# A two-layer block on one core: the end of a projection in another order, one gate's table later, four sums on GpSimd

## The chip, the core and the metric

One core of a Trainium2 chip runs the whole program in one launch. Its engines are TensorE (PE), VectorE (DVE), ScalarE (ACT) and GpSimd (POOL), each with its own list of instructions; SyncE (SP) issues most DMAs, POOL and ACT issue the others. The metric is the device time of one execution in microseconds (us).

## The reference, cut to what matters

The first layer makes 4096 columns of mixed features `y` for 512 tokens, in two halves of 2048 (`y_a` from a state space scan, `y_b` from a gated product), projects them with `w_out` and normalises:

```python
y_a = _rmsnorm(y * jax.nn.silu(z_ssd), g_ssd)
sg = jnp.einsum('gqk,bckgd->bcqgd', w_s, vn) + jnp.swapaxes(b_s, 0, 1)[:, :, None]
y_b = _rmsnorm(u * sg.reshape(bsz, L, MLP_W) * jax.nn.silu(z_mlp), g_mlp)
mixed = jnp.concatenate([y_a, y_b], axis=-1) @ w_out      # 512x4096 @ 4096x2048
out = _rmsnorm(mixed, g_post[l])
x = x + gate[:, None] * out
```

The second layer normalises this `x` again and begins with its own projections.

## The kernel before, in words

All matmuls of size work on float32 numbers split in a high and a low part: ACT writes the high part of a weight tile (`WH`, 128x1024), DVE the rest (`WL`, raw minus high), and TensorE makes three products, high by high, high by low, low by high. Four buffers `WH[n % 4]`, `WL[n % 4]` go round: unit n can be made when TensorE has used unit n-4. `make(u)` in ACT's and DVE's programs makes unit u's part.

**The projection.** K is cut in four blocks of 1024 (`c` = 0 to 3), and the columns in two halves (`q` = 2c + n). For seven of the eight pairs, `q` = 0 to 6, the 2x2 block product is made by Strassen's scheme in the form of Winograd: seven products (`ph` = 0 to 6) in place of eight. One `product(q, ph)` is 24 matmuls of 128x128 by 512 columns, over two units of weights, and it comes in two halves `j` (token blocks), each in a bank of its own. I write (q, ph) for it below. Weight forms (`E`, `F`, `H`, `G`) are sums of raw tiles: `add_load` on POOL issues a DMA from DRAM that adds to the tile in SBUF, as soon as DVE has taken the earlier form's low part from that tile (event `lo`). In POOL's list the order of a group is F, H, G, and then E of the next group, two issues each.

The left side needs forms of `y`: `F` holds the four blocks A11, A21, A12, A22 of one `c`, and four sums of 128x1024, `sum_S(c, 1..4)`, are made in `E0` and `E1s` on DVE: S1 = A21 - A22, S2 = S1 - A11, S4 = A12 + S2, S3 = A11 - A21. ACT splits off the high part (`form_high`, `FH`), DVE the low part (`form_low`, `FL`). Tables (`forms_due`, `sums_due`, `tiles_due`) say in which slot (q, ph) of the engines' lists each stands. In an even group the third sum S3 stands in slot (q, 2) and its form 5 in slot (q, 3); in an odd group S1, S2 and S4 of the next block stand in slots 3, 5 and 6. SP loads the next `y` (`load_y`, eight DMAs F<-SY) when the last forms of the block before have been made, form 6 among them; ACT then scales its tiles.

After each half product its bank is added to `O` in SBUF (`evacuate`, on DVE or, in eight cases, on ACT). The first group also holds the last two of the 16 gates of the first layer. A gate is: SP loads `vg`, `wsg`, `bsg`; DVE scales `wsg` into the table `wsr`; TensorE multiplies it with `vg` (line L841, written `sg`); DVE finishes `sgt` and `evb`; ACT stores them and squares; DVE adds to `GA`. The steps are generators in a queue `bg2`, advanced by `step(bg2, n)`. Gate 15's `wsr` was made in DVE's slot (0, 2), and its matmuls came right after product (0, 2).

**The tail.** The eighth pair is done plainly: eight units `tail_unit(0..7)`, the first four for column block 2 (order: unit, then token block k), the last four for column block 3 with k outermost, so that token block k is complete one after the other. `take_out(nb, k)` adds such a bank to `O`; `square_out(k, nb)` on ACT squares a quarter of a token row block for the norm; `gain(k, nb)` on DVE multiplies by the table `gg`. Then for each k comes the chain `take_out(3, k)`, square, `rx` on POOL, `make_x1` (x + gate * norm), square again, `rx2` on POOL, scale into `XR` (`xs2`). TensorE's transposes of `XR` (L967, `turn_row`) open the second layer. In the loop over `i` of the tail, each step first makes unit i + 2.

Of the kernel before, what the change touches and what calls it, by code (L numbers as in the profile page):

```python
# [153 lines left out]


def sums_due(q, ph):

    c = q // 2
    if q == 0:
        return {0: [(0, 2), (0, 4)], 2: [(0, 3)]}.get(ph, [])  # L160
    if q % 2:
        return [(c + 1, i) for i in {3: [1], 5: [2], 6: [4]}.get(ph, [])]
    return [(c, 3)] if ph == 2 else []
# [320 lines left out]
def tensor_program(P, m, s, ev):  # L484
# [407 lines left out]
    def product(q, ph):  # L892
        for j in range(2):
# [19 lines left out]
            if q == 0:  # L913
                step(bg2)

    for q in range(GROUPS):
        for ph in range(7):
            product(q, ph)
            if q == 0 and ph == 5:
                drain(bg2)  # L920
                b, bank = take(hb, "gate sums")
                P.wait_ge(*at("GA", 15))
                column_sums(b, bank, m.GA, "gate sums")
                drop(hb, b, ("rb sum",))
# [224 lines left out]
def scalar_program(A, m, s, ev, I):  # L1149
# [388 lines left out]
    for q in range(GROUPS):  # L1538
        for ph in range(7):
            u = form_unit(q, ph, 0)  # L1540
            make(u + 2)
            if ph:
                evacuate(q, ph - 1, 1)
            elif q:
                evacuate(q - 1, 6, 1)
            make(u + 3)
            for c, f in forms_due(q, ph):
                form_high(c, f)
            for c, i in tiles_due(q, ph):
                scale_tile(c, i)  # L1550
            if q == 0:
                step(bg2, 2)
                if ph == 5:
                    drain(bg2)
            evacuate(q, ph, 0)
    for i in range(8):
        if i < 6:
            make(tail_unit(i + 2))
        if 1 < i < 4:
            square_out(2 * i - 4, 0)  # L1560
            square_out(2 * i - 3, 0)
        elif 3 < i < 6:
            square_out(2 * i - 8, 1)
            square_out(2 * i - 7, 1)
    for k in range(4):
        square_out(k, 2)
# [241 lines left out]
def vector_program(V, m, s, ev):  # L1808
# [348 lines left out]
    def sum_S(c, i):  # L2157
        A11, A21, A12, A22 = (m.F[:, v] for v in range(4))
        for e in ("y scaled", c, 3), ("y scaled", c, 7):
            V.wait_ge(*at(*e))  # L2160
        if i == 1:
            if c:
                V.wait_ge(*at("fl", c - 1, 3))
                V.wait_ge(*at("fh", c - 1, 3))
            V.then(TT(m.E0, A21, A22, ALU.subtract), "S", c, 1)
        elif i == 2:
            if c:
                V.wait_ge(*at("fl", c - 1, 5))
            V.wait_ge(*at("S", c, 1))
            V.then(TT(m.E1s, m.E0, A11, ALU.subtract), "S", c, 2)  # L2170
        elif i == 3:
            V.wait_ge(*at("fl", c, 4))
            V.then(TT(m.E1s, A11, A21, ALU.subtract), "S", c, 3)
        else:
            V.wait_ge(*at("fl", c, 2))
            V.wait_ge(*at("S", c, 2))
            V.then(TT(m.E0, A12, m.E1s, ALU.add), "S", c, 4)

# [4 lines left out]
    def block(u0):  # L2183
        for k4 in range(4):
# [3 lines left out]
            if u0 + k4 == AT_OUT - 1:  # L2188
                form_low(0, 1)
                sum_S(0, 1)  # L2190
# [91 lines left out]
    for q in range(GROUPS):  # L2282
        for ph in range(7):
# [7 lines left out]
            if q == 0:  # L2291
                step(bg2, 2)
# [245 lines left out]
def gpsimd_program(G, m, s, ev, I):  # L2538
# [613 lines left out]
```

## Time and profile before

| | us |
|---|---|
| median of three runs | 2763.28 (2761.79 to 2767.49) |
| the profiled execution, its own time | 2763.36 |
| its span, first to last instruction | 2761.6 |
| TensorE busy in the span | 2710.3 (98%) |
| ACT, DVE, POOL busy | 1134.6, 1595.0, 371.4 |
[...]

TensorE works nearly all the time, so what another engine saves is worth something only where TensorE waits. The projection runs from about 1434 us to 1763 us of the span.

### The profile page before, as it was taken

The page shows a single profiled execution, that of the slowest core. Times are in us where ns is not written, and L with a number is a line of the kernel's source. Part 1 is how long each engine was busy: PE and PEld are TensorE (multiplying, and loading weights), DVE is VectorE, ACT ScalarE, POOL GpSimd, SP SyncE. Part 2 cuts the span into 40 slices and gives each one's busy share as a digit, 9 for nine tenths or more (in the row PEclk, how much of TensorE's full clock was granted, in tenths as well). Part 3 has the DMA queues.
Part 4 walks back from the last instruction along what each step waited for, and adds up shares of the span by engine and source line. Part 5 has one row for each costly group of instructions (what it writes and reads, how often), then busy time and mean ns, then how long its engine had stood idle before and what let it go on. Part 6 is the DMA issues. An engine that isn't in the chain of part 4 may idle for free. (4 is left out here: it accounts for less than half of the span.)

```text
span 2761.6 us, 32964 instructions
## 1 busy us (share of the span) xinstructions
PE 2710.3 (98%) x12974; PEld 2199.6 (80%) x12974; DVE 1595.0 (58%) x1923; ACT 1134.6 (41%) x1491; POOL 371.4 (13%) x438
## 2 busy tenths in 40 slices
PE   6999999999999999999999999899999999999999
PEld 2688888888888888888887788688887888788787
DVE  2377767755565456676757778634454453533733
ACT  3342222234344333333346554635656643442621
POOL 2101000001334224322301211100000000000000
PEclk8999999999999999999999999999999999999999
DMA  9667766754545554555458988332222223222342
GB/s 398 259 229 263 273 229 257 271 178 140 183 154 166 162 181 138 165 167 182 150 175 231 208 219 220 131 107 84 77 84 84 77 92 101 83 93 99 106 176 92
DMA packets 174313, 461.36 MB, mean 167 GB/s; under 512 B 15440, under 2 KB 68688, under 8 KB 163920
## 3 DMA queue, kind: packets, MB, share of 16 engines
q1 hardware_dynamic: 129616, 309.37, 32.8%
q0 software_dynamic: 21728, 112.91, 14.2%
q10 hardware_dynamic: 22816, 36.97, 3.8%
q8 instruction: 104, 1.70, 0.3%
q14 instruction: 49, 0.40, 0.0%
HBM read 420.13 MB, written 39.06 MB: 166 GB/s over the span
## 5 line engine op out<-in xcount | busy, mean ns | idle before, releaser
L1812 DVE TENSOR_TENSOR WL<-RAW,WH 128x1024 fp32r<-128x1024 f32 (+1 forms) x399 | 487.6, 1230 | 591.8 <-ACT WH L1159 422.5
L523 PE MATMUL PB<-HH,WH 128*128 128x512 f32 x2048 | 817.8, 399 | 2.7 <-DVE WL L1812 2.7
L529 PE MATMUL PB<-HH,WL 128*128 128x512 f32 x2048 | 801.3, 391 | 0.0
L528 PE MATMUL PB<-HL,WH 128*128 128x512 f32 x2048 | 801.2, 391 | 0.0
L1159 ACT ACTIVATE WH<-RAW 128x1024 fp32r<-128x1024 f32 (+1 forms) x399 | 408.4, 1039 | 339.7 <-PE PB L635 111.0
L523 PEld LDWEIGHTS PB<-HH,WH 128*128 128x128 f32 x2048 | 384.9, 188 | 103.9 <-issue 22.9
L529 PEld LDWEIGHTS PB<-HH,WL 128*128 128x128 f32 x2048 | 385.1, 188 | 66.3
L528 PEld LDWEIGHTS PB<-HL,WH 128*128 128x128 f32 x2048 | 385.7, 188 | 65.4 <-issue 3.3
L633 PE MATMUL PB<-WH,HH 128*128 128x512 f32 x768 | 303.0, 394 | 1.6 <-ACT Kr L1159 0.8
L635 PE MATMUL PB<-WH,HL 128*128 128x512 f32 x768 | 299.4, 390 | 0.0
L634 PE MATMUL PB<-WL,HH 128*128 128x512 f32 x768 | 299.2, 390 | 0.0
L1820 DVE SCALAR_TENSOR_TENSOR AACC<-AU,small,AACC 128x2048 f32<-128x2048 f32 x60 | 141.1, 2352 | 72.6 <-DMA AU<-in_w_ada 72.4
L633 PEld LDWEIGHTS PB<-WH,HH 128*128 128x128 f32 x768 | 144.2, 188 | 33.2 <-issue 2.5
L634 PEld LDWEIGHTS PB<-WL,HH 128*128 128x128 f32 x768 | 144.3, 188 | 30.3 <-issue 1.0
L635 PEld LDWEIGHTS PB<-WH,HL 128*128 128x128 f32 x768 | 144.2, 188 | 30.4
L905 PE MATMUL PB<-WH,FH 128*128 128x512 f32 x392 | 155.2, 396 | 3.1 <-DVE O L1820 2.4
L907 PE MATMUL PB<-WL,FH 128*128 128x512 f32 x392 | 155.1, 396 | 0.0
L908 PE MATMUL PB<-WH,FL 128*128 128x512 f32 x392 | 153.6, 392 | 0.0
L2638 POOL TENSOR_TENSOR xw<-xk,wk 128x256 f32<-128x256 f32 x80 | 76.9, 987 | 262.7 <-ACT xk L1159 162.8
L1812 DVE TENSOR_TENSOR WL<-hold,WH 128x1024 fp32r<-128x1024 f32 x67 | 81.6, 1222 | 50.9 <-ACT WH L1159 48.7
L527 PE MATMUL PB<-CL,WH 128*128 128x256 f32 x384 | 108.4, 282 | 0.0
L526 PE MATMUL PB<-CH,WH 128*128 128x256 f32 x384 | 107.8, 281 | 0.0
(346 smaller groups left out, 3351.5 us busy)
## 6 DMA issues: line engine op xcount, KB each, us to landing
RAW<-in_w_in_t SPq DMA_DIRECT2D x312, 512.0 KB, 3.7
AU<-in_w_ada POOLq DMA_DIRECT2D x64, 1024.0 KB, 5.6
RAW<-in_w_out_t SPq DMA_DIRECT2D x47, 512.0 KB, 4.7
hold<-in_w_out_t SPq DMA_DIRECT2D x35, 512.0 KB, 5.8
bcb<-R SPq DMA_DIRECT2D x64, 256.0 KB, 6.2
hold<-in_w_out_t POOLq DMA_DIRECT2D x32, 512.0 KB, 6.6
RAW<-in_w_out_t POOLq DMA_DIRECT2D x24, 512.0 KB, 6.4
S<-so ACTq DMA_DIRECT2D x24, 384.0 KB, 2.5
```

Of the source, the lines that this page charges most:

```text
L523: h.matmul(banks[j], lh, m.HH[:, t, :], start=st, stop=False)
L528: h.matmul(banks[j], lh, m.HL[:, t, :], start=False, stop=False)
L529: ins = h.matmul(banks[j], ll, m.HH[:, t, :], start=False, stop=en)
L633: h.matmul(bank, xh, wh[:, tt, :], start=t == 0, stop=False)
L634: h.matmul(bank, xh, wl[:, tt, :], start=False, stop=False)
L635: ins = h.matmul(bank, xl, wh[:, tt, :], start=False, stop=t == 15)
L905: h.matmul(bank, xh, wh[:, tt, :], start=p == 0 and ph < 3, stop=False, skip_group_check=True)
L907: h.matmul(bank, xh, wl[:, tt, :], start=False, stop=False, skip_group_check=True)
L908: ins = h.matmul(bank, xl, wh[:, tt, :], start=False, stop=p == 3, skip_group_check=True)
L1159: return h.activation(o, a, f, **kw)
L1812: return h.tensor_tensor(o, a, b, op)
L1820: return h.scalar_tensor_tensor(out=o, in0=a, scalar=sc, in1=b, op0=op0, op1=op1)
```

## The change

Three edits. The four sums move from DVE's list to POOL's list. The first group's gate steps are given per slot: gate 15's `wsr` goes from DVE's slot (0, 2) to (0, 3), its matmuls go from behind product (0, 2) to behind product (0, 4), its rest on DVE and ACT to slot (0, 5), and the column sums of `GA` (four small matmuls) from behind (0, 5) to behind (0, 6); the two late `evacuate(0, 3, j)` go to slot (1, 0). And in the tail squares and gains of column blocks 0 and 1 come at once in steps i = 0 to 2, those of block 2 in steps 3 to 5, and between the low part of unit 7 and `take_out(3, 0)` stands one `gain`.

```diff
-def sums_due(q, ph):
-    c = q // 2
-    if q == 0:
-        return {0: [(0, 2), (0, 4)], 2: [(0, 3)]}.get(ph, [])
-    if q % 2:
-        return [(c + 1, i) for i in {3: [1], 5: [2], 6: [4]}.get(ph, [])]
-    return [(c, 3)] if ph == 2 else []
...
@@ tensor_program
-            if q == 0:
+            if q == 0 and ph in (0, 1, 4):
                 step(bg2)
...
-            if q == 0 and ph == 5:
+            if q == 0 and ph == 6:
                 drain(bg2)
...
@@ scalar_program (vector_program has the first two lines too)
-                step(bg2, 2)
+                step(bg2, (2, 2, 0, 1, 1, 0, 0)[ph])
...
-        if 1 < i < 4:
-            square_out(2 * i - 4, 0)
-            square_out(2 * i - 3, 0)
-        elif 3 < i < 6:
-            square_out(2 * i - 8, 1)
-            square_out(2 * i - 7, 1)
-    for k in range(4):
-        square_out(k, 2)
+        if i < 2:
+            for k in 2 * i, 2 * i + 1:
+                square_out(k, 0)
+                square_out(k, 1)
+        elif i == 3:
+            square_out(0, 2)
+            square_out(1, 2)
+        elif i == 4:
+            square_out(2, 2)
+            square_out(3, 2)
...
@@ vector_program
-            for c, i in sums_due(q, ph):
-                sum_S(c, i)
-            if (q, ph) == (0, 6):
-                for late in 1, 3:
-                    evacuate(0, late, 0)
-                    evacuate(0, late, 1)
+            if (q, ph) in ((0, 6), (1, 0)):
+                for j in range(2):
+                    evacuate(0, 3 if q else 1, j)
...
-        if i > 3:
-            take_out(2, i - 4)
-            gain(i - 4, 0)
-            gain(i - 4, 1)
-    for k in range(4):
-        gain(k, 2)
+        if i in (1, 2):
+            for k in 2 * i - 2, 2 * i - 1:
+                gain(k, 0)
+                gain(k, 1)
+        elif i == 3:
+            for k in range(3):
+                take_out(2, k)
+        elif i == 4:
+            take_out(2, 3)
+            for k in range(3):
+                gain(k, 2)
+        elif i == 5:
+            gain(3, 2)
...
@@ gpsimd_program (sum_S as it was, with G.wait_ge and h.tensor_tensor)
+        elif i == 3:
+            G.wait_ge(*at("fl", c, 4))
+            G.then(h.tensor_tensor(m.E1s, A11, A21, ALU.subtract), "S", c, 3)
...
+    sum_S(0, 1)
     sum_E(0)
+    sum_S(0, 2)
+    sum_S(0, 4)
     for q in range(GROUPS):
         sum_F(q)
+        if q % 2 == 0:
+            sum_S(q // 2, 3)
         sum_H(q)
         sum_G(q)
+        if q % 2:
+            for i in 1, 2, 4:
+                sum_S(q // 2 + 1, i)
         if q + 1 < GROUPS:
             sum_E(q + 1)
```

What this does to the lists is seen at three places. **POOL, first group.** Before; the issues are two each of E (`RAW_53`, `RAW_54`), F (the same tiles), H (`hold_187`, `hold_188`):

```order
L2671 TENSOR_SCALAR small<-small 128x4
L2676 DMA RAW_53<-in_w_out_t 128x1024
L2676 DMA RAW_54<-in_w_out_t 128x1024
L2676 DMA RAW_53<-in_w_out_t 128x1024
L2676 DMA RAW_54<-in_w_out_t 128x1024
L2676 DMA hold_187<-in_w_out_t 128x1024
L2676 DMA hold_188<-in_w_out_t 128x1024
```

and after the change (`E_185` is `E0`):

```order
L2644 TENSOR_SCALAR small<-small 128x4
L2676 TENSOR_TENSOR E_185<-F 128x1024
L2649 DMA RAW_53<-in_w_out_t 128x1024
L2649 DMA RAW_54<-in_w_out_t 128x1024
L2681 TENSOR_TENSOR E1s<-E_185,F 128x1024
L2688 TENSOR_TENSOR E_185<-F,E1s 128x1024
L2649 DMA RAW_53<-in_w_out_t 128x1024
L2649 DMA RAW_54<-in_w_out_t 128x1024
L2684 TENSOR_TENSOR E1s<-F 128x1024
L2649 DMA hold_187<-in_w_out_t 128x1024
L2649 DMA hold_188<-in_w_out_t 128x1024
```

The first three sums stand around the issues of E; S3 stands between the issues of F and those of H, so H is issued only after S3, which itself waits for form 4's low part.

**DVE, the tail.** Before, from the low part of unit 5 on (`WL_63`; those of units 6 and 7 are `WL_60` and `WL_61`):

```order
L1812 TENSOR_TENSOR WL_63<-hold_190,WH_59 128x1024
L1812 TENSOR_TENSOR WL_60<-hold_187,WH_56 128x1024
L1820 SCALAR_TENSOR_TENSOR O<-PB,small,O 128x512
L1812 TENSOR_TENSOR O<-O,gg 128x512 x2
L1812 TENSOR_TENSOR WL_61<-hold_188,WH_57 128x1024
L1820 SCALAR_TENSOR_TENSOR O<-PB,small,O 128x512
L1812 TENSOR_TENSOR O<-O,gg 128x512 x2
L1820 SCALAR_TENSOR_TENSOR O<-PB,small,O 128x512
L1812 TENSOR_TENSOR O<-O,gg 128x512 x2
L1820 SCALAR_TENSOR_TENSOR O<-PB,small,O 128x512
L1812 TENSOR_TENSOR O<-O,gg 128x512 x6
L1820 SCALAR_TENSOR_TENSOR O<-PB,small,O 128x512
```

and after, from the low part of unit 4 (`WL_62`) on:

```order
L1804 TENSOR_TENSOR WL_62<-hold_189,WH_58 128x1024
L1804 TENSOR_TENSOR O<-O,gg 128x512 x4
L1804 TENSOR_TENSOR WL_63<-hold_190,WH_59 128x1024
L1812 SCALAR_TENSOR_TENSOR O<-PB,small,O 128x512 x3
L1804 TENSOR_TENSOR WL_60<-hold_187,WH_56 128x1024
L1812 SCALAR_TENSOR_TENSOR O<-PB,small,O 128x512
L1804 TENSOR_TENSOR O<-O,gg 128x512 x3
L1804 TENSOR_TENSOR WL_61<-hold_188,WH_57 128x1024
L1804 TENSOR_TENSOR O<-O,gg 128x512
L1812 SCALAR_TENSOR_TENSOR O<-PB,small,O 128x512
```

`take_out(2, k)` and `take_out(3, k)` are the rows O<-PB; the gains are O<-O,gg. The last gains stood between unit 7's low part and the last O<-PB; now one is left there, but three `take_out` stand ahead of unit 6's low part and one more with three gains ahead of unit 7's.

**ACT, the tail.** Before, from unit 2's high part (`WH_56`) to that of unit 7 and the squares behind it:

```order
L1159 ACTIVATE WH_56<-hold_187 128x1024
L1159 ACTIVATE WH_57<-hold_188 128x1024
L1159 ACTIVATE WH_58<-hold_189 128x1024
L1159 ACTIVATE jk,small<-O 128x512 x2
L1159 ACTIVATE WH_59<-hold_190 128x1024
L1159 ACTIVATE jk,small<-O 128x512 x2
L1159 ACTIVATE WH_56<-hold_187 128x1024
L1159 ACTIVATE jk,small<-O 128x512 x2
L1159 ACTIVATE WH_57<-hold_188 128x1024
L1159 ACTIVATE jk,small<-O 128x512 x7
```

and after:

```order
L1149 ACTIVATE WH_56<-hold_187 128x1024
L1149 ACTIVATE jk,small<-O 128x512 x4
L1149 ACTIVATE WH_57<-hold_188 128x1024
L1149 ACTIVATE jk,small<-O 128x512 x4
L1149 ACTIVATE WH_58<-hold_189 128x1024
L1149 ACTIVATE WH_59<-hold_190 128x1024
L1149 ACTIVATE jk,small<-O 128x512 x2
L1149 ACTIVATE WH_56<-hold_187 128x1024
L1149 ACTIVATE jk,small<-O 128x512 x2
L1149 ACTIVATE WH_57<-hold_188 128x1024
L1149 ACTIVATE jk,small<-O 128x512
```

The squares (jk,small<-O) of the first two column blocks now stand around unit 3's high part, and two pairs, which wait for DVE's `take_out(2, k)`, stand ahead of those of units 6 and 7.

## Rows read from the trace of the kernel before

**Rows 1.** The page, its head and part 1 (busy us, share, instructions):

```profile
span 2761.6 us, 32964 instructions
PE 2710.3 (98%) x12974; PEld 2199.6 (80%) x12974; DVE 1595.0 (58%) x1923; ACT 1134.6 (41%) x1491; POOL 371.4 (13%) x438
```

**Rows 2.** Waits of TensorE, 1400 to 1900 us (total us, times, longest):

```profile
PE PB L967 <- ACT XR L1159: 11.9, 2, 8.2
PE PB L841 <- DVE wsr L1816: 4.6, 2, 3.9
PE PB L905 <- DVE O L1820: 2.4, 2, 1.6
```

**Rows 3.** The timeline of PE (start us, duration, what, [idle before]):

```profile
1452.54 0.40 PE L908 MATMUL PB<-WH,FL 128*128 128x512 f32 x1
1456.87 2.05 PE L841 MATMUL PB<-wsr,vg 128*128 128x128 f32 x8 [3.93 <-DVE wsr L1816]
1458.57 0.77 PE L905 MATMUL PB<-WH,FH 128*128 128x512 f32 x1
...
1499.12 0.40 PE L905 MATMUL PB<-WH,FH 128*128 128x512 f32 x1
...
1578.55 0.50 PE L905 MATMUL PB<-WH,FH 128*128 128x512 f32 x1 [1.63 <-DVE O L1820]
```

**Rows 4.** Stretches: length, busy by engine, granted clock, DMA, GB/s:

```profile
1456.80:1458.90 2.10, 2.03 (x9) 2.06 (x10) 2.06 (x2) 0.00 (x0) 0.00 (x0) 0.50 1.07 277
1458.90:1460.50 1.60, 1.60 (x6) 1.26 (x5) 1.60 (x3) 1.06 (x1) 0.00 (x0) 0.61 1.09 228
1560.00:1580.00 20.00, 18.37 (x79) 14.45 (x78) 13.80 (x15) 12.68 (x15) 3.49 (x4) 1.00 0.88 213
```

**Rows 5.** The timelines of DVE and POOL in the first group:

```profile
1440.38 1.22 DVE L1812 TENSOR_TENSOR E1s<-E,F 128x1024 f32<-128x1024 f32 x1
1455.85 0.88 DVE L1816 TENSOR_SCALAR wsr<-wsg,small 128x128 f32<-128x128 f32 x4 [4.09 <-DMA wsg<-in_w_s_t]
...
1452.05 0.87 POOL L2676 DMA_DIRECT2D hold<-in_w_out_t  x1 [0.27 <-DVE WL L1812]
```

**Rows 6.** DMA issues, 1451.8 to 1452.5, then 1535.5 to 1536 us:

```profile
hold<-in_w_out_t POOLq DMA_DIRECT2D x1, 512.0 KB, 12.5
...
hold<-in_w_out_t POOLq DMA_DIRECT2D x1, 512.0 KB, 7.4
```

**Rows 7.** The timeline of SP's queue (start us, duration, issues):

```profile
1469.11 5.11 SPq L2745 DMA_DIRECT2D F<-SY  x8
...
1548.37 5.31 SPq L2745 DMA_DIRECT2D F<-SY  x8
```

**Rows 8.** Two POOL lines and one DVE line (ns min/median/max):

```profile
L2665 POOL TENSOR_TENSOR YA<-YA,ysq x16: 1273/1296/1432, 733.3 to 1379.4; 128x512 f32<-128x512 f32 x16
L2658 POOL TENSOR_TENSOR Sst<-Sst,htmp x64: 723/744/1702, 687.2 to 1340.3; 128x256 f32<-128x256 f32 x64
L1812 DVE TENSOR_TENSOR WL<-RAW,WH x399: 681/1224/1796, 44.0 to 2736.9; 128x1024 fp32r<-128x1024 f32 x192, 128x512 fp32r<-128x512 f32 x8
```

**Rows 9.** The timeline of ACT in the third group:

```profile
1542.32 1.06 ACT L1159 ACTIVATE WH<-hold 128x1024 fp32r<-128x1024 f32 x1 [2.11 <-PE PB L908]
```

**Rows 10.** The timelines of DVE, ACT and PE in the tail:

```profile
1738.51 1.28 DVE L1812 TENSOR_TENSOR O<-O,gg 128x512 f32<-128x512 f32 x2
1751.41 0.75 DVE L1820 SCALAR_TENSOR_TENSOR O<-PB,small,O 128x512 f32<-128x512 f32 x1
1768.01 0.74 DVE L1820 SCALAR_TENSOR_TENSOR O<-PB,small,O 128x512 f32<-128x512 f32 x1
...
1729.05 0.64 ACT L1159 ACTIVATE jk<-O 128x512 f32<-128x512 f32 x1
1741.12 1.06 ACT L1159 ACTIVATE WH<-hold 128x1024 fp32r<-128x1024 f32 x1 [3.13 <-PE PB L948]
...
1745.07 0.39 PE L946 MATMUL PB<-WH,FH 128*128 128x512 f32 x1
```

More of the change, by code:

```diff
@@ L2155, in vector_program @@
     bg, bg2 = deque([scans()]), deque()
[L2157 to L2177, printed above, removed]
     def form_low(c, f):
@@ L2189, in block @@
                 form_low(0, 1)
-                sum_S(0, 1)
                 form_low(0, 2)
@@ L2291, in vector_program @@
             if q == 0:
-                step(bg2, 2)
+                step(bg2, (2, 2, 0, 1, 1, 0, 0)[ph])
                 if ph == 5:
@@ L2693, in sum_G, with sum_S @@
         add_load(q, 6, 4, 1, 0, 1, "G")
+    def sum_S(c, i):
+        A11, A21, A12, A22 = (m.F[:, v] for v in range(4))
+        for e in ("y scaled", c, 3), ("y scaled", c, 7):
+            G.wait_ge(*at(*e))
+        if i == 1:
+            if c:
+                G.wait_ge(*at("fl", c - 1, 3))
+                G.wait_ge(*at("fh", c - 1, 3))
+            G.then(h.tensor_tensor(m.E0, A21, A22, ALU.subtract), "S", c, 1)
+        elif i == 2:
+            if c:
+                G.wait_ge(*at("fl", c - 1, 5))
+            G.wait_ge(*at("S", c, 1))
+            G.then(h.tensor_tensor(m.E1s, m.E0, A11, ALU.subtract), "S", c, 2)
+        elif i == 3:
+            G.wait_ge(*at("fl", c, 4))
+            G.then(h.tensor_tensor(m.E1s, A11, A21, ALU.subtract), "S", c, 3)
+        else:
+            G.wait_ge(*at("fl", c, 2))
+            G.wait_ge(*at("S", c, 2))
+            G.then(h.tensor_tensor(m.E0, A12, m.E1s, ALU.add), "S", c, 4)
+    sum_S(0, 1)
     sum_E(0)
+    sum_S(0, 2)
+    sum_S(0, 4)
     for q in range(GROUPS):
         sum_F(q)
+        if q % 2 == 0:
+            sum_S(q // 2, 3)
         sum_H(q)
         sum_G(q)
+        if q % 2:
+            for i in 1, 2, 4:
+                sum_S(q // 2 + 1, i)
         if q + 1 < GROUPS:
```

## The prediction

> **What bounds the kernel now.** I read the page first: TensorE is busy 98% of the span, DVE 58%, POOL 13% [rows 1]. So the 16 sums of about 1.2 us that leave DVE are worth nothing as such; only waits of TensorE count. The chain of waits for the stretch that the change touches names three: 11.9 us at the transposes that open the second layer, 4.6 us for the tables `wsr` (one of 3.9), and 2.4 us for evacuations [rows 2]. The reader should see that the first two are just where two of the edits are. The timeline of TensorE gives the places: product (0, 2) issues its last matmul at 1452.54, gate 15's matmuls wait 3.93 us and start at 1456.87, product (0, 3) starts at 1458.57 [rows 3]. [...]
>
> A product takes 5.56 us: from (1, 3) at 1499.12 to (3, 3) at 1578.55 are 14, less the wait of 1.63 [rows 3].
>
> **Edit 1, gate 15 later.** The table `wsr` waited for its DMA until 1455.85 [rows 5]. Behind product (0, 4) its matmuls are wanted at about 1452.8 + 2 x 5.56 = 1463.9, eight us after that landing, so the wait of 3.93 goes. With it go the low clock's losses: the gate's matmuls took 1.70 us (1456.87 to 1458.57) and need half, 0.85, and the next 1.6 us at 0.61 lost 0.6. Together 5.4 us: (0, 5) could start at 1463.9 + 0.9 = 1464.8. The gate itself still costs its 0.85, later. Its stores and `GA` now stand in slot (0, 5); TensorE wants `GA` only behind (0, 6), 11 us on. The moved `evacuate(0, 3, j)` is wanted at (1, 2), two products after its slot: nothing.
>
> **Edit 2, the sums on POOL.** Price of one: POOL took 1.296 us for 512 columns and 0.744 for 256 [rows 8], 2.16 ns a column; 1024 columns make 1.296 + 512 x 2.16 = 2.4 us. Upper bound: the 256-column addition also took 1.702 us when DVE worked beside it, four times that is 6.8. DVE pays too: its 1.224 us subtraction went up to 1.796 [rows 8]. I take 3.0 us, since around the sum that matters DVE has only one such instruction. [...]
>
> Where it hurts is POOL's order, because it issues the weight adds. In group 0, S3 waits for form 4's low part and H is queued behind S3. DVE's list reaches that low part as follows: product (0, 1) ends at 1452.8 - 5.6 = 1447.2, which frees the slot of (0, 3)'s second unit; ACT's high part 1.06 [as rows 9], DVE's low part 1.22, form 4's low part 1.22 bring 1450.9 (before, it stood behind the late table). S3 ends at about 1454.0; H's second issue follows at 1455.1, against 1452.05 [rows 5]. Three us later, but its landing need not be: at 1452.05 it took 12.5 us beside the loads of F, `wsg` and B21; the like issue in the third group took 7.4 [rows 6]. DVE's two sums ahead of form E's low parts are gone (the first stood at 1440.38 [rows 5]), so F is issued some 2.3 us sooner, into an idle stretch, and is out of the way. I take 7.4: H is complete at 1462.5, before at 1464.55.
>
> What H holds up is more than (0, 5): ACT makes form 6 behind it, and SP loads the next `y` when form 6's low part is done. From landing to that: 1.06 + 1.22 + 1.22 = 3.5 us at least, 4.6 in the trace (1464.55 to 1469.11 [rows 7]); I take 3.9, so `y` starts at 1466.4. And `y` sets the next group: (1, 3) started 30.0 us after it, (3, 3), which did wait, 30.2 us after its own at 1548.37 [rows 3, 7]. So (1, 3) starts at 1496.4, although TensorE could be there at 1464.8 + 0.5 (ACT's evacuation of (0, 4) behind H) + 1.0 (`GA` sums: 40.55 us from (0, 3) to (1, 3) less seven products and 0.6 of low clock) + 5 x 5.56 = 1494.1. Against 1499.12 the first part is worth **2.7 us**, not 5.4: half of the gain is given back at (1, 2) or (1, 3) as a wait for weights that landed beside `y`. Bounds: 5.4, and with 12.5 us for H: 1467.6, `y` 1471.5, (1, 3) 1501.5, a loss of 2.4.
>
> From group 1 on: in even groups H goes out about 1 to 2 us later. ACT waits 2.11 us for TensorE's slot before it makes H [rows 9], and slot to need is 1.4 + 5.6 us, of which 1.06 + 1.22 + 0.3 are used: 4.4 us of cover, and without it each us late costs one in three groups. In odd groups three sums stand between G's second issue and E's first. These lie 2.75 products apart, 15.3 - 0.9 = 14.4 us; three sums of 3 to 4 us fit. The waits of 1.63 and 0.8 at (3, 3) and (5, 3) stay.
>
> **Edit 3, the tail.** TensorE is on time; the chain is late: token block 0 of the last column block is complete at 1745.07 + 1.4 + 0.25 = 1746.7 (0.25 is the handoff: unit 3 ended 3 x 1.4 ahead of 1745.07, and ACT took its slot at 1741.12), `take_out(3, 0)` starts at 1751.41, the fourth at 1768.01, 16.6 us later [rows 10]; the XR's at the end follow. DVE spends the 4.7 us between on gains (0.64 us each [rows 10]) and `take_out`s. After the change this is done before, but units 6 and 7 now stand behind pairs that wait. Step by step (handoffs 0.05 to 0.1): a tile of a tail unit is 1.40 us, the unit 5.6. ACT: `take_out(2, 1)` has its bank at 1745.07 - 5 x 1.40 = 1738.1 and is done at 1739.1, its square 1739.95, unit 6's high part 1741.05; DVE: unit 6's low part 1742.35, `take_out(2, 3)` 1743.05; ACT: square until 1743.9 (0.64 [rows 10] and some 0.2 for the reading of its sum), unit 7's high part 1744.95, before it started at 1741.12; DVE: low part 1746.3. TensorE wants unit 7 at 1745.07 [rows 10], so a new wait of 1.3 us. Block 0 is complete at 1748.05, one gain has fitted in, and the chain runs its 16.6 us: 1764.65, where TensorE's own end, (1746.7 + 3 x 5.5) + 1.3 = 1764.5, is the same. Shift **3.2 us** (bounds: 0 if TensorE or ACT slips by three more, 4.7 if unit 7 is in time). Squares and gains of the first steps stand in ACT's and DVE's free time; unit 3 is 2.8 us later but wanted 12 us on.
>
> **The sum.** The profiled execution took 2763.36 us (0.08 over the median; 1.8 outside its span). 2763.36 - 2.7 - 3.2 = 2757.5.
>
> **Rivals.** (B) H lands late, 12.5 us after its issue: 2763.36 + 2.4 - 3.2 = 2762.6. For it: the trace's own issue took that long; against: fewer transfers lie beside. (C) The tail gives nothing, its wait at unit 7 growing to 4.5 us, as ACT and DVE hand over six times there: 2760.7. (D) Slower: POOL beside a busy DVE needs so long for a sum that E of the even groups is late. With t each the wait is 3t - 14.4 - 4.4 in three groups; at t = 7.6 that is 12.0, and S3 delays (1, 3) to 1501.0: 2763.36 + 12.0 + 1.9 - 3.2 = 2774. It decides against the change from t = 7.1 on; the dearest bound from rows is 6.8. (E) Group 1 isn't held by `y`: 2763.36 - 5.4 - 3.2 = 2754.8. For it: (1, 3) showed no wait before, so 30.0 is only an upper bound.
>
> **Numbers.** Forecast 0.47 (own range 2754.5 to 2759.5), B 0.20, C 0.12, D 0.06, E 0.15. A measurement tells 0.2%, 5.5 us, from nothing: faster is below 2757.8. Of the forecast's chance 0.28 lies there, with E 0.43; slower is D; the rest, 0.51, is within. The range 2753.8 to 2762.8 leaves out D, a part of B and a little of E.
>
> **What would show it.** Right: gate 15's matmuls start without a wait near 1464; (0, 5) at 1464.8 to 1466; F<-SY about 1466; a new wait of 1 to 3 us at (1, 2) or (1, 3); POOL's sums of 2.4 to 4 us; a wait near 1.3 us at unit 7 of the tail; `take_out(3, 0)` 3.2 us earlier in relation to the tail's first matmul; the waits for XR down from 11.9 to about 9. Wrong: H's second landing after 1465, sums over 4.8 us, a wait for E in groups 2, 4 or 6, or a new drop of the granted clock in one of the new waits, which I priced at nothing since 1.63 us brought none.

## The result and the profile after

The changed kernel took 2766.39 us (median of 20 runs, 2764.11 to 2773.15) against 2762.73 us (20 runs, 2759.89 to 2767.49): the ratio is 1.0013, with a 95% interval of 1.0007 to 1.0019. It is slower by 3.7 us, which is within the 0.2% that I had called no change, and outside my range of 2753.8 to 2762.8.

The profiled execution of the changed kernel took 2771.42 us, 5.0 more than its median, so its trace shows some microseconds that are its own; some of them are named below. The page, its head and part 1, beside [rows 1]:

```profile
span 2769.2 us, 32976 instructions
PE 2715.4 (98%) x12974; PEld 2200.6 (79%) x12974; DVE 1601.2 (58%) x1907; ACT 1132.5 (41%) x1491; POOL 412.3 (15%) x454
```

DVE lost 16 instructions of 1.22 us, 19.5 us of work, and is busy 6.2 us more. This is the first sign: what is left on it has become slower. The waits of TensorE from 1425 to 1830 us, beside [rows 2]:

```profile
PE PB L895 <- DVE O L1812: 9.9, 9, 2.9
PE PB L957 <- ACT XR L1149: 7.6, 1, 7.6
PE PB L831 <- DVE wsr L1808: 2.0, 1, 2.0
PE PB L936 <- DVE WL L1804: 0.7, 1, 0.7
```

The gate's wait of 3.9 is gone, the wait for XR is 4.3 shorter, and the waits for evacuations (`O`) went from 2.4 us in two to 9.9 us in nine. Their places, on PE's timeline (the first is the first product's first matmul, 1434.06 before; the last but one is unit 7 of the tail):

```profile
1436.39 0.51 PE L895 MATMUL PB<-WH,FH 128*128 128x512 f32 x1 [0.69 <-ACT evb L1149]
1467.54 1.05 PE L831 MATMUL PB<-wsr,vg 128*128 128x128 f32 x8
1469.06 0.50 PE L895 MATMUL PB<-WH,FH 128*128 128x512 f32 x1 [0.46 <-ACT t L1149]
1477.68 0.79 PE L895 MATMUL PB<-WH,FH 128*128 128x512 f32 x1 [2.89 <-DVE O L1812]
1515.98 0.49 PE L895 MATMUL PB<-WH,FH 128*128 128x512 f32 x1 [1.02 <-DVE O L1812]
1522.25 0.50 PE L895 MATMUL PB<-WH,FH 128*128 128x512 f32 x1 [0.29 <-DVE O L1812]
1757.44 0.47 PE L936 MATMUL PB<-WH,FH 128*128 128x512 f32 x1 [0.69 <-DVE WL L1804]
1783.86 0.90 PE L957 MATMUL PB<-cst,XR 128*128 128x128 f32 x3 [7.61 <-ACT XR L1149]
```

To find where the time went I took the start of each product's first matmul on this timeline, counted from the first product of the same trace, in both kernels. The changed kernel is ahead by 4.45 us at (0, 3) (5.8 but for 1.35 that it loses at (0, 1)), by 1.38 at (0, 6), and behind by 2.19 at (1, 0), by 4.37 at (2, 0), 6.55 at (4, 0) and 9.20 at (6, 0). So groups 1, 3 and 5 add 2.2, 2.2 and 2.7 us, nearly all behind their products 4, and groups 2 and 4 as good as nothing. From the tail's first matmul to the end of the span it takes 1039.1 us (2769.2 - 1730.1) and before 1043.0 (2761.6 - 1718.6): 3.9 us given back. So there are three questions: why the gate's gain is gone at (1, 0), what the odd groups lose, and whether the tail is understood.

**The odd groups.** POOL's and DVE's timelines in group 1:

```profile
1508.07 2.75 POOL L2676 TENSOR_TENSOR E<-F 128x1024 f32<-128x1024 f32 x1
1510.96 3.21 POOL L2681 TENSOR_TENSOR E1s<-E,F 128x1024 f32<-128x1024 f32 x1
1517.13 3.32 POOL L2688 TENSOR_TENSOR E<-F,E1s 128x1024 f32<-128x1024 f32 x1 [2.96 <-DVE FL L1804]
```

```profile
1509.24 6.02 DVE L1804 TENSOR_TENSOR WL<-hold,WH 128x1024 fp32r<-128x1024 f32 x2 [2.35 <-ACT WH L1149]
1515.19 0.73 DVE L1812 SCALAR_TENSOR_TENSOR O<-PB,small,O 128x512 f32<-128x512 f32 x1
1515.85 1.21 DVE L1804 TENSOR_TENSOR FL<-E,FH 128x1024 fp32r<-128x1024 f32 x1
1516.98 1.21 DVE L1804 TENSOR_TENSOR WL<-hold,WH 128x1024 fp32r<-128x1024 f32 x1
1518.11 0.73 DVE L1812 SCALAR_TENSOR_TENSOR O<-PB,small,O 128x512 f32<-128x512 f32 x1
1518.78 2.76 DVE L1804 TENSOR_TENSOR WL<-hold,WH 128x1024 fp32r<-128x1024 f32 x1
```

Two low parts take 6.02 us instead of 2.4. The pair ends 1.1 us after the second sum (1514.17), and the low part begun at 1518.78 ends 1.1 us after the third (1520.45). Both ends fit an instruction that does its 1.2 us of work only once the sum is over. The other way round, the low part begun at 1516.98 kept its 1.21 beside the third sum, and that sum took 3.32, where S3 takes 2.4. The `O<-PB` at 1518.11, which reads one operand from PSUM, took its 0.73 while the third sum ran. The evacuation at 1515.19 came late, and TensorE waits for it until 1515.98. The two waits of TensorE here are 1.3 of the 2.1 us that products 4 to 6 lose; the rest are longer steps between the matmuls around them. From these rows I took a theory for the runs below to test, **Port**: of a POOL sum and a DVE instruction that both have two inputs in SBUF, the one that comes second waits for the other to end (6.02 us instead of 2.4 and 2.76 instead of 1.21 on DVE, 3.32 instead of 2.4 on POOL). The rival, **Order**: what is late comes of lists, forms that wait for POOL's sums, or E's loads queued behind them.

**The gate.** DVE's and ACT's timelines in slot (0, 5), and the stretches with the granted clock:

```profile
1473.73 0.74 DVE L1812 SCALAR_TENSOR_TENSOR sgt<-PB,par,bsg 128x512 f32<-128x512 f32 x1
1474.51 0.69 DVE L1804 TENSOR_TENSOR evb<-sgt,evb 128x512 f32<-128x512 f32 x1
1476.28 0.69 DVE L1804 TENSOR_TENSOR GA<-GA,sgt 128x512 f32<-128x512 f32 x1 [1.07 <-ACT sgt L1149]
1476.88 0.74 DVE L1812 SCALAR_TENSOR_TENSOR O<-PB,small,O 128x512 f32<-128x512 f32 x1
```

```profile
1463.96 1.06 ACT L1149 ACTIVATE WH<-hold 128x1024 fp32r<-128x1024 f32 x1 [4.73 <-DMA hold<-in_w_out_t]
1466.42 1.06 ACT L1149 ACTIVATE WH<-hold 128x1024 fp32r<-128x1024 f32 x1 [1.40 <-DMA hold<-in_w_out_t]
```

```profile
1477.50:1480.00 2.50, 2.32 (x6) 1.84 (x7) 2.50 (x4) 1.86 (x3) 0.87 (x1) 0.50 1.00 335
1480.00:1484.00 4.00, 4.00 (x12) 3.14 (x11) 1.87 (x3) 0.69 (x1) 0.88 (x1) 0.55 1.06 399
```

`evacuate(0, 5, 0)` (the last row of DVE) is behind the gate's rest in slot (0, 5), which waits for ACT's square. Product (0, 6) needs its bank: 2.89 us of wait, and then a granted clock of 0.50 and 0.55. From (0, 3) to (1, 0) the changed kernel takes 30.4 us, before it was 23.8: the gain of 5.8 is given back in full, nearly all of it at this one place.

### The profile page after: what moved, and what is told of

It is laid out like the page before. It is cut to its first block and busy times, and to the rows that moved or that the text cites. A ratio compares the mean times of both kernels' runs of the same rounds, so it can differ in the third digit from the quotient of the medians.

```text
span 2769.2 us, 32976 instructions
## 1 busy us (share of the span) xinstructions
PE 2715.4 (98%) x12974; PEld 2200.6 (79%) x12974; DVE 1601.2 (58%) x1907; ACT 1132.5 (41%) x1491; POOL 412.3 (15%) x454
## 5 line engine op out<-in xcount | busy, mean ns | idle before, releaser
L1804 DVE TENSOR_TENSOR WL<-hold,WH 128x1024 fp32r<-128x1024 f32 x67 | 101.2, 1511 | 42.3 <-ACT WH L1149 39.0
```

The costliest lines, as they stand in the source:

```text
L1804: return h.tensor_tensor(o, a, b, op)
```

## The experiments

Fourteen kernels ran. The last three columns of this table come from each kernel's profiled execution, worked out as above: the start of (1, 0) after the first product; the three products from (q, 4) to (q + 1, 0) in groups 1, 3 and 5; and from the tail's first matmul to the end of the span. In groups 2 and 4 those three products took 16.52 or 16.53 us with every kernel, but 17.1 in pieces256, group 4.

| kernel | ratio to before (95%) | (1, 0) | groups 1, 3, 5 | tail to end |
|---|---|---|---|---|
| before | | 48.3 | 16.5, 16.5, 16.5 | 1043.0 |
| changed | 1.0013 (1.0007 to 1.0019) | 50.5 | 18.6, 18.9, 18.8 | 1039.1 |
| tail_only | 0.9986 (0.9977 to 0.9995) | 47.7 | 16.5, 16.5, 16.5 | 1039.1 |
| sums_only | 1.0032 (1.0019 to 1.0044) | 50.6 | 18.8, 18.8, 18.8 | 1042.9 |
| gate_only | 1.0005 (0.9996 to 1.0014) | 49.7 | 16.5, 17.9, 16.6 | 1042.9 |
| odd_on_dve | 0.9984 (0.9975 to 0.9993) | 48.7 | 16.5, 16.6, 16.5 | 1039.1 |
| pieces256 | 1.0008 (0.9999 to 1.0017) | 48.4 | 17.9, 18.2, 18.2 | 1039.6 |
| evac_first | 1.0009 (1.0001 to 1.0018) | 46.7 | 18.6, 18.8, 18.8 | 1039.4 |
| extra_two | 1.0041 (1.0028 to 1.0054) | 48.5 | 18.8, 20.8, 21.4 | 1042.8 |
| extra_one | 1.0002 (0.9993 to 1.0011) | 47.6 | 17.9, 16.6, 16.6 | 1042.9 |
| best2 | 0.9985 (0.9976 to 0.9994) | 49.4 | 16.5, 16.5, 16.5 | 1038.2 |
| best3 | 0.9983 (0.9974 to 0.9992) | 49.3 | 16.5, 16.5, 16.5 | 1038.1 |
| tail_fix | 0.9983 (0.9974 to 0.9991) | 47.5 | 16.5, 16.5, 16.5 | 1038.5 |
| best4 | 0.9975 (0.9964 to 0.9986) | 45.9 | 16.5, 17.0, 17.1 | 1038.5 |
| gate_fixed | 0.9993 (0.9984 to 1.0002) | 44.9 | 17.4, 16.9, 16.8 | 1043.0 |
| best5 | 0.9971 (0.9960 to 0.9982) | 44.9 | 16.5, 16.5, 16.5 | 1038.0 |

A single execution scatters: without any edit before (1, 0), tail_only and tail_fix have 47.7 and 47.5 there against 48.3, and gate_only, with its sums on DVE, has 17.9 in group 3. I read differences of 1.5 us and more from one trace, smaller ones only where they come again in several groups or kernels or from the ratios, whose intervals reach 1.7 to 3.6 us to either side.

**One edit at a time.** Three kernels have one of the three edits each; their diffs are the parts of the diff above.

> The kernel before with the change of the tail alone (squares, gains and take_outs of the last column blocks in the new order). From the trace of the changed kernel, where the chain from the last tail product to the XR transposes shrank from 13.4 to 8.7 us and unit 7 of the tail waited 0.69 us: 3.8 us faster than before (2.8 to 4.5). My prediction's term was 3.2. The rival, that the tail's shift came only because TensorE arrived late there (it stood 9.2 us further on), gives less than 1 us.

It took 2759.16 us against 2763.38, 4.2 faster. The last column gave 3.9, with TensorE where it is before: the tail's gain does not hang on TensorE being late.

> The kernel before with the four sums of y's blocks on GpSimd alone. Theory Port: while a GpSimd sum runs, an instruction of VectorE with two inputs in SBUF stands still until the sum is over, so WL is up to 3.3 us late in groups 1, 3 and 5: +2.2 us each at (odd, 5) and (odd, 6), +1.35 us at (0, 1), together 7.5 to 10 us slower than before; VectorE rows of WL<-hold of 2.5 us and more in the odd groups. Theory Order (the price of a sum is only its own time on GpSimd, what is late comes of the order of the lists): within 1 us of before but for the +1.35 us at (0, 1).

It took 2772.42, 9.0 slower: inside Port's 7.5 to 10, not Order's 1, but only in part for Port's reason. The 1.35 us at (0, 1) that I had read from the changed kernel's trace as the price of S1 ahead of E's adds did not come again (0.31 here, 0.6 and less in the others with sums on POOL), so that belonged to the one execution. The odd groups lost 2.3 us each, 6.9 in all, which is Port's. The rest, 2.3 us at (1, 0) in its trace, came of the order of the lists in the first group: the wait for `wsr` behind (0, 2) shrank to 1.38, but S3 took 4.45 us, H, which stands behind it, went out at 1457.87, and at (0, 5) TensorE waited 4.34 for `t` (the tile into which ACT takes the bank of (0, 4)), with the granted clock at 0.50 after it. That the two add up to the middle of the range is luck.

> The kernel before with gate 15 one product later alone. Theory Behind (the evacuation of (0, 5) stands behind the rest of the gate on VectorE): product (0, 3) starts 5 to 6 us earlier, and most of it goes again at (0, 6), with a wait of TensorE for O of 2 to 3.5 us there and a granted clock of 0.5 to 0.6 behind it: between 1 us faster and 1.5 us slower than before. Theory Late H (the give-back comes of S3 on GpSimd, which sends H's loads out 3 us later): without the sums on GpSimd the gain stays, 4 to 5.5 us faster, and no wait for O at (0, 6).

It took 2764.15, 0.8 slower, the interval reaching from 1.1 faster to 3.9 slower. (0, 3) is 5.9 us earlier (1.7 of it is the gate's matmuls, which now come behind (0, 4)), (1, 0) 1.4 later. This is what Behind had: the wait for `O` at (0, 6), the low clock, the gain gone. Late H expected no such wait with the sums on DVE and a gain of 4 to 5.5 us, and is wrong. But Behind had not all of it either: there are two waits, one for `t` at (0, 5), one for `O` at (0, 6). PE's timeline and the stretches:

```profile
1469.40 0.50 PE L905 MATMUL PB<-WH,FH 128*128 128x512 f32 x1 [2.42 <-ACT t L1159]
1478.03 0.79 PE L905 MATMUL PB<-WH,FH 128*128 128x512 f32 x1 [2.89 <-DVE O L1820]
```

```profile
1469.00:1472.00 3.00, 2.60 (x11) 2.17 (x12) 2.50 (x3) 2.10 (x4) 0.00 (x0) 1.00 0.22 43
1478.00:1481.00 3.00, 2.97 (x7) 2.40 (x8) 3.00 (x4) 1.71 (x3) 0.88 (x1) 0.50 1.04 389
```

The three together: 9.0 + 0.8 - 4.2 = 5.6 us, the change 3.7. They add up within their intervals.

**What the sums cost.** First the odd groups' sums back on DVE, in the slots of before (`sums_due` with its line for odd q):

```diff
-        if q % 2:
-            for i in 1, 2, 4:
-                sum_S(q // 2 + 1, i)
@@ vector_program
+            for c, i in sums_due(q, ph):
+                sum_S(c, i)
```

> The changed kernel with the sums S1, S2 and S4 of the odd groups back on VectorE (group 0's four sums and S3 of groups 2 and 4 stay on GpSimd). Theory Port: the 2.1 to 2.3 us at (1, 5)+(1, 6), (3, 5)+(3, 6) and (5, 5)+(5, 6) are gone, 6.5 us less than the changed kernel, so about 3 us faster than before. Theory Order with the loads of E held by the sums as the cause gives the same 6.5 us here, and is told apart by the run with sums in pieces. If neither holds, within 1 us of the changed kernel.

It took 2759.62 against 2763.38, 3.8 faster, so the change without these nine sums is 7.4 us faster than with them. The three odd groups are back at 16.5. The seven sums that stayed on POOL cost nothing measurable with this order (3.8 faster is about what the tail and gate edits give together, 4.2 less 0.8; in sums_only, with the gate's old order, S3 had its part in a loss), although DVE is held by them as well: low parts (`WL<-hold`) from 1490 to 1700 us took 1332 ns on average, 1222 before.

The second kernel keeps the order and cuts each sum into four:

```diff
+    def pieces(out, a, b, op, *key):
+        for p in range(4):
+            G.then(h.tensor_tensor(out[:, p], a[:, p], b[:, p], op), *(key if p == 3 else ()))
-            G.then(h.tensor_tensor(m.E0, A21, A22, ALU.subtract), "S", c, 1)
+            pieces(m.E0, A21, A22, ALU.subtract, "S", c, 1)
...
```

> The changed kernel with each of GpSimd's sums made as four instructions of 256 columns instead of one of 1024, in the same places of GpSimd's list. Theory Port: VectorE's instruction with two inputs in SBUF waits only until the piece that runs is over (0.7 us), so WL<-hold in group 1 is late by 0.7 us at most instead of 3, and the 2.2 us in groups 1, 3 and 5 go: 5 to 6.5 us less than the changed kernel. Theory Order (the loads of E stand behind three sums on GpSimd, or the forms behind late sums): the sums take as long or longer, so the same time as the changed kernel or up to 2 us more.

It took 2764.59, a ratio 0.0005 below that of the change: some 1.4 us, not 5 to 6.5, and the two intervals overlap. The odd groups lost 1.3 to 1.7 instead of 2.1 to 2.3. Both point Port's way, and the size isn't Port's. POOL's and DVE's timelines in group 1 show why:

```profile
1504.05 3.14 POOL L2670 TENSOR_TENSOR E<-F 128x256 f32<-128x256 f32 x4
1507.33 5.61 POOL L2670 TENSOR_TENSOR E1s<-E,F 128x256 f32<-128x256 f32 x4
1513.08 4.60 POOL L2670 TENSOR_TENSOR E<-F,E1s 128x256 f32<-128x256 f32 x4
...
1505.22 4.74 DVE L1804 TENSOR_TENSOR WL<-hold,WH 128x1024 fp32r<-128x1024 f32 x2 [2.36 <-ACT WH L1149]
1510.55 1.80 DVE L1804 TENSOR_TENSOR FL<-E,FH 128x1024 fp32r<-128x1024 f32 x1
1512.27 1.76 DVE L1804 TENSOR_TENSOR WL<-hold,WH 128x1024 fp32r<-128x1024 f32 x1
1514.61 1.77 DVE L1804 TENSOR_TENSOR WL<-hold,WH 128x1024 fp32r<-128x1024 f32 x1
```

The first DVE row holds two instructions; the first of them alone is

```profile
1505.22 3.06 DVE L1804 TENSOR_TENSOR WL<-hold,WH 128x1024 fp32r<-128x1024 f32 x1 [2.36 <-ACT WH L1149]
```

It got no turn between the pieces: it ended 1.1 us after the fourth piece of the first sum (1507.19), as if that sum were whole. The other four take turns with the pieces. Each waits for one (some 0.55 us: 1.76 to 1.80 instead of 1.21), and each meets one, since the second and third sum are drawn out to 5.6 and 4.6 us. The five low parts took 10.1 us, and in the change 11.2 (6.02, 1.21, 1.21 and 2.76). Cutting changes who waits, and little of how much, in this group; the others I did not go through row by row.

The third and fourth take the dependence away. They are the kernel before, with all sums on DVE, and three more POOL instructions where the change has its sums, into a buffer that nobody reads, with an input of `m.F`. In both, E's loads stand behind them as they do behind the change's sums, and SP's later loads into `F` and `XR` wait for them too:

```diff
+        G.then(h.tensor_tensor(m.scr, A21, A22, ALU.subtract), "extra", c, i)      (extra_two)
+        G.then(h.tensor_scalar(m.scr, A21, -1.0, None, ALU.mult), "extra", c, i)   (extra_one)
...
         sum_G(q)
+        if q % 2:
+            for i in 1, 2, 4:
+                extra(q // 2 + 1, i)
```

> The kernel before, all its sums on VectorE, with three more instructions of 128x1024 with two inputs on GpSimd in the odd groups, where the changed kernel has its sums; they write an unused buffer and no engine of the product path waits for them. Theory Port: they hold VectorE's instructions with two inputs in SBUF up all the same, WL<-hold takes 2.5 us and more in groups 1, 3 and 5, and the kernel is 5 to 10 us slower than before. Theory Order (what is late comes of forms that wait for GpSimd's sums): nothing waits for these, so within 1 us of before; but the loads of E, which still stand behind them, could cost up to 2 us in a group under this theory, with WL<-hold at 1.2 us.

> The same with three instructions of 128x1024 with one input on GpSimd in the same places (and the same wait in front of E's loads). Theory Port, if it is the second read of SBUF that shuts VectorE out: no row of VectorE grows by more than 0.2 us, within 1 us of before. If any instruction of GpSimd does it: 3 to 8 us slower. If it is E's loads behind them: the same loss as with two inputs, scaled by their duration.

With two inputs it took 2774.24 against 2762.77, 11.5 slower; with one, 2762.90, the same (1.9 faster to 3.0 slower). This settles what the odd groups lose: no form waits for the extra instructions, and E's loads stand behind both kinds, which run 3.09 and 3.24 us on average. Order's loads would have cost the same in both. DVE's timeline in extra_two, group 1:

```profile
1504.73 5.98 DVE L1813 TENSOR_TENSOR WL<-hold,WH 128x1024 fp32r<-128x1024 f32 x2 [1.24 <-ACT WH L1160]
1514.23 2.76 DVE L1813 TENSOR_TENSOR WL<-hold,WH 128x1024 fp32r<-128x1024 f32 x1
```

These are the change's 6.02 and 2.76 again. In groups 3 and 5 it loses 4.3 and 4.9 us, more than the change, as DVE has its own sums to make besides (`E<-F`, 4.1 us in both instead of 1.22). For extra_one my line of 0.2 us for DVE's rows was wrong:

```profile
1502.40 1.61 DVE L1813 TENSOR_TENSOR WL<-hold,WH 128x1024 fp32r<-128x1024 f32 x1 [0.92 <-ACT WH L1160]
1504.86 2.02 DVE L1813 TENSOR_TENSOR WL<-hold,WH 128x1024 fp32r<-128x1024 f32 x1 [0.85 <-ACT WH L1160]
...
1582.05 2.74 DVE L1813 TENSOR_TENSOR E<-F 128x1024 f32<-128x1024 f32 x1
```

One input holds DVE up too, by 0.4 and 0.8 us in group 1 and by 1.5 in group 3 (last row; the same in group 5), and not for its whole 3 us. In its one trace group 1 lost 1.3 us, with a wait of 0.54 for `O` at (1, 6), groups 3 and 5 nothing, and the median shows no loss. Port would hold each DVE instruction for at most a sum's length (2.75 to 3.32 us in group 1 of the change), and the traces agree for two inputs (6.02 for two, 2.76 for one, instead of 1.21 each); for one input they show less than the whole instruction (at most 1.5 us of 3.12). Which of two starts first can't be told from the rows' starts here: `E<-F` of extra_two in group 3 begins at 1585.77, 0.29 us ahead of POOL's instruction (1586.06), and was held all the same.

**What takes the gate's gain.** The first edit moves one line of DVE in the changed kernel:

```diff
-                if ph == 5:
-                    drain(bg2)
...
                 evacuate(q, ph, 0)
+            if (q, ph) == (0, 5):
+                drain(bg2)
```

> The changed kernel with VectorE taking the first unit of product (0, 5) out of PSUM before the rest of gate 15 instead of behind it. If the rest of the gate is what holds (0, 6) up, TensorE's wait of 2.89 us for O there is gone and with it the low clock behind it (1.5 to 2 us): 3.5 to 5 us less than the changed kernel. If the late landing of H is what holds (0, 6) up, through the high and low parts that VectorE makes first, a wait of 1.5 us or more stays and the gain is under 1.5 us.

(0, 6) started 3.1 us earlier than in the change, counted from (0, 5), as expected, but a wait of 2.35 for `O` came half a product later and the low clock again (0.56), and (1, 0) kept 1.7 of it. The ratio is 1.0009 to the change's 1.0013; their intervals overlap, so the medians show no gain; the trace has 1.7 us, below the 3.5 expected. What is late next is ACT, whose timeline here is:

```profile
1474.81 0.63 ACT L1149 ACTIVATE sgt<-evb 128x512 f32<-128x512 f32 x1 [3.77 <-DVE evb L1804]
1475.35 1.99 ACT L1149 ACTIVATE WH<-hold 128x1024 fp32r<-128x1024 f32 x2
```

ACT's square of the gate waits 3.77 us for DVE; the high parts for (1, 0) are behind it, their low parts stand ahead of `evacuate(0, 5, 1)` on DVE, and the second half of (0, 6) needs that one.

Next, the sums on DVE, the tail mended (below) and this order (best2), then with the first unit of (0, 4) taken out ahead of H's second unit on ACT (best3):

```diff
+            if (q, ph) == (0, 4):
+                evacuate(0, 4, 0)
             make(u + 3)
```

> The kernel before with gate 15 a product later, the first unit of (0, 5) taken out ahead of the gate's rest, the new tail with the last square and the gains of the third column block behind unit 7, and all sums on VectorE as before. From the parts: tail 3.8 + 0.7 for the wait at unit 7, gate 5.9 less the 2.4 us wait for H and its low clock (1.0): 7 us faster than before (6 to 8.5). If the gate's gain is lost in any case to the loads of H and y, 4.5 us faster.

> As the kernel of the line before, and ScalarE takes the first unit of product (0, 4) out before it makes H's second unit, for which it waits 1.8 us for the load. If that order is what makes TensorE wait 2.4 us for t at (0, 5), the wait goes or shrinks below 0.5: 1.5 to 3.4 us less than without. If H's second load itself sets the pace, TensorE waits for WL half a product later instead: within 1 us of it.

They took 2758.05 and 2758.06 against 2762.68: 4.6 faster both, which is the tail alone. So "the gate's gain is lost in any case" held for these orders. In best3 the wait for `t` is gone (0.9 us for WL in its place), and (0, 5) starts 2.7 us earlier; (1, 0) is where it was. Here a wait taken away ahead of a later one was worth nothing.

The gate's rest split (best4), and VectorE's evacuation moved once more (best5); gate_fixed is best5 without the new tail:

```diff
@@ scalar_program
+            if (q, ph) == (0, 5):
+                drain(bg2)
             make(u + 3)
@@ vector_program
+            if (q, ph) == (0, 5):
+                step(bg2, 1)               (sgt and evb, ahead of the slot)
             make(u + 2)
...
+            if (q, ph) == (0, 5):
+                evacuate(0, 5, 0)          (best5, gate_fixed)
             make(u + 3)
```

> The kernel before with gate 15 later, the new tail with unit 7 mended, (0, 4) taken out early on ScalarE, and the gate's rest split: VectorE makes sgt and evb at the start of slot (0, 5), ScalarE stores and squares them between the two units of (0, 6), VectorE adds to GA behind the evacuation of (0, 5). If the gate's rest is what costs the 5 us between (0, 6) and (1, 0), these go: (1, 0) starts 3 us or more earlier than before, and the kernel is 7.5 to 10 us faster than before. If the loads of weights (H, then the units of group 1) set the pace there, waits for WL take its place: 4.5 to 5.5 us faster, which is the tail alone.

> As the kernel with the gate's rest split (best4), and VectorE takes the first unit of (0, 5) out before it makes the second unit of (0, 6), not behind it. Order of the lists as the cause: TensorE's wait of 1.75 us for O at (0, 6) is gone, (1, 0) starts 4 to 4.5 us earlier than before instead of 2.4, and the kernel is 8.5 us faster than before (7.5 to 10). The loads as the cause: a wait for WL or for ScalarE's O takes its place by (1, 1), (1, 2) or (1, 3), and the kernel stays at 6.6 us (5.5 to 7.4).

> The kernel before with gate 15 a product later and all three changes of order around it (the first units of (0, 4) and (0, 5) taken out early, the gate's rest split), and the old tail. Order as the cause: 3.5 to 4.5 us faster than before, against 0.8 us slower with the gate later alone. The loads as the cause: 1 to 2.5 us faster.

best4 took 2756.13 against 2762.77, 6.6 faster, between its two ranges, with (1, 0) 2.4 us earlier, not 3. best5 took 2754.54 against 2761.68, 7.1 faster. Its expectation had 7.5 to 10 for Order and 5.5 to 7.4 for loads; the median is in the second range, but its interval (5.0 to 11) doesn't tell these apart. Its trace does in part, with PE's timeline at (0, 5) and (0, 6) and the stretch around them:

```profile
1464.56 0.47 PE L905 MATMUL PB<-WH,FH 128*128 128x512 f32 x1 [0.84 <-DVE WL L1818]
1472.71 0.50 PE L905 MATMUL PB<-WH,FH 128*128 128x512 f32 x1 [0.67 <-DVE O L1826]
```

```profile
1452.00:1487.00 35.00, 33.46 (x151) 26.50 (x151) 21.73 (x27) 20.48 (x25) 4.38 (x5) 1.00 0.97 270
```

The granted clock stays at 1.00, and (1, 0) starts 3.4 us earlier than before instead of later, though not the 4 to 4.5 of Order. gate_fixed has (1, 0) at the same place, 3.3 us earlier, but took 2759.38, 2.3 faster (4.4 faster to 0.6 slower), inside what I had set for loads (1 to 2.5). In its trace 2.4 us go again by (4, 0), among them a wait of 0.27 for `O` at (1, 3); best5, with the same order up to there, loses 0.1. Why, I can't say from one trace each. That the order in slot (0, 5) takes the gain is shown by where (1, 0) starts (1.4 us later with gate_only, 2.4, 3.4 and 3.3 earlier in best4, best5 and gate_fixed); the medians point the same way (gate_fixed 2.3 faster, gate_only 0.8 slower), with intervals that overlap. What keeps the rest of the gain is not shown. The loads have a part in it: ACT took H's second unit up 30.5 us after the first product in best5, having waited 1.25 for it, as in gate_only (30.6), and the 0.84 for `WL` is that unit's.

**The tail mended.** Last, the square and the gains of block 2 behind unit 7:

```diff
@@ scalar_program
             square_out(2, 2)
-            square_out(3, 2)
+        elif i == 5:
+            square_out(3, 2)
@@ vector_program
             take_out(2, 3)
-            for k in range(3):
-                gain(k, 2)
         elif i == 5:
-            gain(3, 2)
+            for k in range(4):
+                gain(k, 2)
```

> The kernel before with the new tail alone, and in it the last square and the gains of the third column block behind unit 7 on ScalarE and VectorE. The wait of 0.69 us at unit 7 goes: 4.5 us faster than before (3.8 to 5.2). If the chain from the last tail product sets the end either way, the same 3.8 to 4.2 us as with the tail of the change.

It took 2757.66 against 2762.77, 5.1 faster (2.5 to 7.2). The wait at unit 7 is gone, and the last column has 1038.5 instead of 1039.1. The medians can't show so little: tail_only's 4.2 lies inside this interval.

## Why the prediction was wrong

It was 2757.5, and the kernel took 2766.39. Two terms of its sum failed. The first part (gate and first group) stood in it with 2.7 us gained, and gate_only was 0.8 slower. The sums of the odd groups stood in it with nothing, and cost 7.4. The tail stood in it with 3.2 and gave 4.2. 0.8 + 7.4 - 4.2 is 4.0 us slower, and the change was 3.7 slower. By its own steps:

- **Price of a sum on POOL, 2.4 to 3.0 us: right, within 0.2.** The four kinds took 2.4 to 3.2 us on average in the changed kernel.
- **"DVE pays too: its 1.224 us subtraction went up to 1.796": this is the step that failed.** I named the effect and gave it no term in the sum. And the 0.57 us of that row is no price for sums of 1024 columns, since it came of a POOL instruction of 256. The trace of before has both, first DVE's row, then POOL's:

```profile
1330.03 1.80 DVE L1812 TENSOR_TENSOR WL<-RAW,WH 128x1024 fp32r<-128x1024 f32 x1 [2.07 <-ACT WH L1159]
...
1330.00 0.74 POOL L2658 TENSOR_TENSOR Sst<-Sst,htmp 128x256 f32<-128x256 f32 x1
```

DVE's ended 1.1 us after POOL's (1331.83 and 1330.74), so the pattern could have been read there. pieces256 shows the same 0.55 with 256 columns, and the change has 1.5 us on one low part and 3.6 on two together with 1024. I named no instruction of DVE that would stand beside the sums of the odd groups, and set them at nothing because "three sums of 3 to 4 us fit": they fit POOL's list, and what counted was DVE's. It cost 7.4 us (odd_on_dve against the change), twice what the kernel lost in all.
- **Rival D had the sign and another mechanism.** It made E late from 7.1 us a sum. Sums took 2.4 to 3.3 and E was in time.
- **Gate 15: "Together 5.4 us": right**, with 3.93 of wait and 0.85 + 0.6 for the granted clock of 0.50 and 0.61 in [rows 4] (in gate_only (0, 5) would start 5.6 us earlier but for its new wait of 2.42). **"Its stores and `GA` now stand in slot (0, 5)": priced by when TensorE wants `GA`, not by what stands behind them.** Behind them stood `evacuate(0, 5, 0)`: 2.89 us of wait and 3.0 us of low clock (2.32 x 0.5 + 4.0 x 0.45). I expected half of the gain to stay, for another reason (`y`, below), and none did.
- **A new drop of the granted clock** was on my list of what would make it wrong, and came (0.50 and 0.55 behind the 2.89 us).
- **H lands at 1462.5, 28.4 us after the first product: 1.6 us too early.** ACT took its second unit up at 1466.42, 30.0 after; before it landed at 30.5. Its second issue, at 1457.64, took 8.8 us, not 7.4 and not the 12.5 of before: right in kind, and the later issue cost nothing. In gate_only H was issued at 1452.98 and 1454.11, 16.8 and 17.9 us after the first product, and its second unit was taken up 30.6 after; in the change POOL issued H from 1457.05 on, 20.7 after, and it was taken up 30.0 after. In gate_only the DMA engines were at a share of 1.07 from 1460 to 1466.
- **y sets (1, 3), 30.0 us after its loads: wrong.** In best5 (1, 3) started 27.8 us after (1465.58 to 1493.38) without a wait, in gate_fixed 28.1 with one of 0.27. So 30.0 was no bound, and in this point rival E was right. In the change TensorE reached (1, 3) 33.8 us after the loads, without a wait: it was late from slots (0, 5) and (0, 6), not from `y`.
- **The tail: shift 3.2, measured 3.8** (`take_out(3, 0)` at 1751.41 - 1718.60 = 32.8 us after the tail's first matmul, and at 1759.13 - 1730.13 = 29.0). The wait at unit 7 was 0.69, not 1.3. The steps were right; by the prediction's own times (1748.05 against 1751.41) the shift would be 3.4, and what is left is the shorter wait.

The profiled execution of the change shows two losses besides, 1.35 us at (0, 1) and 2.3 us ahead of the projection. The first came to 0.5 at most in the others. The second is scatter: the first product starts anywhere from 1430.5 to 1437.9 us in these traces, latest in best2, which has its sums on DVE. The medians do without both.

## What to carry to other kernels

Before work goes from VectorE to GpSimd, list the VectorE instructions with two inputs in SBUF that will run beside it, and take a price for each from a pair of the same length in a trace: here one of 1.22 us took up to 4.1 beside POOL instructions of 3.09 us on average (extra_two), and the 0.57 us of a pair with 256 columns on POOL would have told too little. In this kernel the seven sums outside the odd groups cost nothing measurable, and the nine in the odd groups, where evacuations stand behind the held instructions, 7.4 us. When a wait is moved to a later slot, read down the lists of all engines in that slot: the evacuation behind the moved work cost as much as the wait had (2.89 us and 3.0 of low clock for the gain of 5.8), and each order that freed one wait showed the next.

## What the runs showed of the hardware

- In the change, two `WL<-hold` beside two POOL sums took 6.02 us instead of 2.4, and both ended 1.1 us after a sum's end; with one SBUF input on POOL the delay was 0.4, 0.8 and 1.5 us (extra_one), and an instruction that read one operand from PSUM had none (0.73 us at 1518.11 in the change).
- The wait of 3.93 us in the trace of before was followed by a granted clock of 0.50 over 2.1 us and 0.61 over the next 1.6, and around its wait of 1.63 us the clock was 1.00 [rows 3, 4]. TensorE's wait of 2.42 us in gate_only left it at 1.00, and the wait of 2.89 us 8.6 us later was followed by 0.50. The length of the wait alone doesn't tell: in evac_first 2.35 us was followed by 0.56.
- H issued 3.9 us later (20.7 instead of 16.8 us after the first product) had landed no later (30.0 and 30.6 after it).
